# Counting row, rows of x and picked indices read from PSUM in the expert search of a decoder step, with a third buffer for U

## The reference

```
q      = x_t @ w_q                                  # two halves of 128
s1, s2 = scores of the halves against 128 keys each
(s1,i1), (s2,i2) = top 16 of each;  c = top 16 of the 256 sums s1 + s2
e      = 128 * i1 + i2                              # expert, one of 16384
g      = softmax(c)
out_t  = sum over the 8*16 picks of  g * gelu(u[e] . x_t) * v[e]
```

## Time and profile before

| | us |
|---|---|
| median of three runs | 3584.55 (3582.04 to 3585.8) |
| the profiled execution | 3597.29, with a span of 3595.5 |
| PE busy | 3243.4 (90%) |
| DVE busy | 1916.3 (53%) |
| ACT busy | 1366.5 (38%) |
| POOL busy | 1044.5 (29%) |

### The profile page before, as it was taken

One profiled execution on the slowest core, in us unless ns is written; L12 is line 12 of the kernel. 1 busy time (PEld: TensorE's weight loads), 2 busy tenths in 40 slices (PEclk: granted clock), 3 DMA queues, 4 the chain that ended last, 5 costly groups with the idle time before them and its releaser, 6 DMA issues. The chain is left out here.

```text
span 3595.5 us, 53340 instructions
## 1 busy us (share of the span) xinstructions
PE 3243.4 (90%) x21256; PEld 3009.4 (84%) x21256; DVE 1916.3 (53%) x2438; ACT 1366.5 (38%) x1708; POOL 1044.5 (29%) x537
## 2 busy tenths in 40 slices
PE   7999997968879888499979998988888999999998
PEld 6999996757778788499979998988888978888886
DVE  5344443432311000465355888887898567777765
ACT  5333322113522232343334444465676433333332
POOL 0000000004532353000023888877667601111100
PEclk9999997668988798799989999998999999999999
DMA  6555552325453542366765788778777978888864
GB/s 203 173 165 165 165 165 87 105 74 169 146 171 132 176 142 78 119 204 203 180 132 141 177 225 205 202 209 247 244 198 240 304 282 316 295 322 296 304 238 152
DMA packets 446567, 696.65 MB, mean 194 GB/s; under 512 B 30205, under 2 KB 342813, under 8 KB 418878
## 3 DMA queue, kind: packets, MB, share of 16 engines
q1 hardware_dynamic: 397086, 554.35, 49.4%
q10 hardware_dynamic: 40128, 73.42, 7.3%
q0 software_dynamic: 9216, 67.11, 4.8%
HBM read 627.94 MB, written 63.70 MB: 192 GB/s over the span
## 5 line engine op out<-in xcount | busy, mean ns | idle before, releaser
L2422 POOL TENSOR_TENSOR peer_uT_low<-peer_uT,peer_uT_high 128x1024 fp32r<-128x1024 f32 x256 | 680.8, 2683 | 316.1 <-ACT peer_uT_high L2449 314.7
L961 POOL TENSOR_TENSOR gate_low<-gate_raw,gate_high 128x512 fp32r<-128x512 f32 x192 | 244.9, 1301 | 1177.1 <-ACT gate_high L917 1177.0
L2325 PE MATMUL banks<-x_high,peer_uT_high 128*128 128x256 f32 x2048 | 515.3, 291 | 22.9 <-ACT peer_picks_T L2479 13.3
L2326 PE MATMUL banks<-x_low,peer_uT_high 128*128 128x256 f32 x2048 | 508.7, 288 | 0.0
L2325 PEld LDWEIGHTS banks<-x_high,peer_uT_high 128*128 128x128 f32 x2048 | 403.7, 197 | 24.6 <-ACT peer_uT_high L2449 19.0
L2326 PEld LDWEIGHTS banks<-x_low,peer_uT_high 128*128 128x128 f32 x2048 | 402.4, 196 | 0.0
L2574 DVE STREAM_TRANSPOSE peer_uT<-peer_u 128x1024 f32<-128x1024 f32 x256 | 310.7, 1229 | 149.5 <-DMA peer_u<-in_peer_u_dram 141.2
L228 PE MATMUL banks<-x_high,win_high 128*128 128x288 f32 (+1 forms) x1312 | 349.1, 296 | 0.0
L229 PE MATMUL banks<-x_low,win_high 128*128 128x288 f32 (+1 forms) x1312 | 348.7, 295 | 0.0
L2449 ACT ACTIVATE peer_uT_high<-peer_uT 128x1024 fp32r<-128x1024 f32 x256 | 265.0, 1056 | 204.4 <-DVE peer_uT L2574 203.1
L198 ACT ACTIVATE win_high<-win_raw 128x2048 fp32r<-128x2048 f32 x84 | 160.8, 1914 | 334.9 <-DVEq L191 329.4
(11 more groups left out here) (377 smaller groups left out, 6891.3 us busy)
## 6 DMA issues: line engine op xcount, KB each, us to landing
win_raw<-in_w_in_dram SPq DMA_DIRECT2D x38, 2048.0 KB, 8.1
peer_u<-in_peer_u_dram SPq DMA_DIRECT2D x256, 256.0 KB
peer_u<-in_peer_u_dram ACTq DMA_DIRECT2D x256, 256.0 KB
peer_u<-in_peer_v_dram SPq DMA_DIRECT2D x64, 1024.0 KB, 5.2
peer_area<-in_peer_v_dram SPq DMA_DIRECT2D x64, 1024.0 KB, 5.4
gate_raw<-in_w_in_dram SPq DMA_DIRECT2D x96, 512.0 KB, 3.9
w_raw<-in_w_up_ret_dram SPq DMA_DIRECT2D x8, 2048.0 KB, 9.5
w_raw<-in_w_out_dram SPq DMA_DIRECT2D x8, 2048.0 KB, 8.1
```

The source lines that it names most:

```text
L961: pool.tensor_tensor(self.low[:, p % 2, c, :, :], self.raw[:, p % 4, :, c * P:(c + 1) * P], self.high[:, p % 2, c, :, :], ALU.subtract).th ...
L2325: pe.matmul(out, UH[:, c, k, :], XH[:, k, 0:DENSE], start=(k == 0), stop=False)
L2326: pe.matmul(out, UH[:, c, k, :], XL[:, k, 0:DENSE], start=False, stop=False)
L2422: pool.tensor_tensor(UL[:, m % 2, part, :], UT[:, m % 2, part, :], UH[:, m % 2, part, :], ALU.subtract).then_inc(low, 1)
```

## The change

- x's rows are copied by ACT once, in block 28, into banks 0 to 3 (PXROWS); the dots read them there. The SBUF space that they leave becomes a third buffer of U from block 30 on (`THIRD_FROM`), so that a load is issued three blocks ahead of its use.
- The counting row is copied once to bank 7 (PIOTA), and the list IXF is written to bank 7. DVE's comparisons, products and hot rows read these from PSUM.
- The plain one-hots move from ACT (five instructions for a spread) to DVE (one 128x512 comparison). The weighted ones are made by `tensor_scalar` instead of `scalar_tensor_tensor`.
- All spreads go to bank 6, so a spread waits until the one before it is kept. Of two spreads in a block the second stands between the high and the low matmuls.
- The first dots lie in halves 64 to 129 instead of 52 to 129. PE waits for all dots ahead of the output stage, which writes banks 0 to 3.

```
-DOTS = ((52, 130, SLOTS * 3 // 16), (130, 248, SLOTS - SLOTS // 8 if SPARSE > NEW else SLOTS))
+THIRD_FROM = 30
+DOTS = ((64, 130, SLOTS * 3 // 16), (130, 248, SLOTS))
...
+        def u_block(m):
+            slot = m % 2 if m < THIRD_FROM else m % 3
+            return (U[:, slot, :] if slot < 2 else XROWS).rearrange("p (E d) -> p E d", E=4)
+        PXROWS = PS[:, 0:4, :].rearrange("p b n -> p (b n)")
+        PIOTA, IXF = PS[:, 7, 0:P], PS[:, 7, P:P + GR * TOPK].rearrange("p (g k) -> p g k", k=TOPK)
...
+        def u_loads_after(m):
+            if m < THIRD_FROM:
+                return [m + 2]
+            return [n for n in ((m + 2, m + 3) if m == THIRD_FROM else (m + 3,)) if n < BLOCKS]
...
@@ spread (PE)
-                    pe.wait_ge(w_ready, after(q - 1))
+                    pe.wait_ge(w_ready, after(q))
...
@@ hidden (PE)
                         pe.matmul(out, UH[:, c, k, :], XL[:, k, 0:DENSE], start=False, stop=False)
+                    for q in between:
+                        spread(q)
...
-                    for q in spread_at(m):
+                    for q in spread_at(m)[:1]:
                         spread(q)
-                    hidden(m // 2, m % 2)
+                    hidden(m // 2, m % 2, spread_at(m)[1:])
...
@@ scalar
-                def second(q):
...
+                act.activation(PIOTA, iota[:], ACT.Copy).then_inc(iota_ready, 1)
...
+                                act.activation(PXROWS, XROWS, ACT.Copy).then_inc(xrows_moved, 1)
...
@@ dot (DVE)
-                    dve.tensor_tensor_reduce(out=ROWS[:, g % 4, :], in0=ROWS[:, g % 4, :], in1=XROWS, scale=1.0, scalar=0.0,
+                    dve.tensor_tensor_reduce(out=ROWS[:, g % 4, :], in0=ROWS[:, g % 4, :], in1=PXROWS, scale=1.0, scalar=0.0,
...
@@ hot_rows (DVE)
                     dve.wait_ge(placed, after(q - 1))
+                    dve.tensor_tensor(SECOND[:, b, :, :], PIOTA.unsqueeze(1).to_broadcast([P, 4, P]),
+                                      SEL[:, 1, 4 * q:4 * q + 4].unsqueeze(2).to_broadcast([P, 4, P]),
+                                      ALU.is_equal).then_inc(second_ready, 1)
                     for j in range(4):
                         t = 4 * q + j
-                        ins = dve.scalar_tensor_tensor(out=FIRST[:, b, j, :], in0=iota[:], scalar=SEL[:, 0, t:t + 1],
-                                                       in1=SEL[:, 2, t:t + 1].to_broadcast([P, P]), op0=ALU.is_equal, op1=ALU.mult)
+                        ins = dve.tensor_scalar(FIRST[:, b, j, :], PIOTA, SEL[:, 0, t:t + 1], SEL[:, 2, t:t + 1],
+                                                ALU.is_equal, ALU.mult)
```

More of the change, by code:

```diff
@@ L2176, in peer @@
         SECOND, FIRST = (shared[:, k * 8 * P:(k + 1) * 8 * P].rearrange("p (b j n) -> p b j n", b=2, j=4) for k in range(2))
-        temporaries = itertools.accumulate((0, 256, 256, 256, 128, 128, 256, 256, 128), lambda at, n: at + n, initial=A_MU)
-        next(temporaries)
-        BEST, IX, IXF = (view(next(temporaries), (GR, TOPK), "p (g k) -> p g k", k=TOPK) for _ in range(3))
+        temporaries = itertools.accumulate((256, 256, 128, 128, 256, 256, 128), initial=A_MU)
+        BEST, IX = (view(next(temporaries), (GR, TOPK), "p (g k) -> p g k", k=TOPK) for _ in range(2))
         TS, J = (view(next(temporaries), (PEER_HEADS, TOPK), "p (h k) -> p h k", k=TOPK) for _ in range(2))
@@ L2218, in peer @@
             "second_ready", "first_ready", "placed", "weights_ready", "weights_stored")
-        turned, uT_high, low, hidden_done, gelu_ready, distances = st.sems(
-            "turned", "uT_high", "uT_low", "hidden_done", "gelu_ready", "distances")
+        turned, uT_high, low, hidden_done, gelu_ready, iota_ready, xrows_moved = st.sems(
+            "turned", "uT_high", "uT_low", "hidden_done", "gelu_ready", "iota_ready", "xrows_moved")
         u_loaded = st.sems(*(f"u_loaded{r}" for r in range(4)))
@@ L2242, in _, with load_u @@
             def _(sp):
-                def load_u(m):
-                    sp.wait_ge(turned, after(2 * (m - 2) + 2))
+                def load_u(m, turned_block):
+                    if m == THIRD_FROM + 2:
+                        sp.wait_ge(xrows_moved, after(1))
+                    sp.wait_ge(turned, after(2 * turned_block + 2))
                     load_quadrants(sp, m, (0, 1))
@@ L2260, in store_gelu @@
                     sp.dma_start(S["gelu"][m], GE[:, m % 4, :]).then_inc(ge_stored[m % 4], 16)
-                load_u(0)
+                load_quadrants(sp, 0, (0, 1))
                 sp.dma_start(iota[:], C["iota"]).then_inc(iota_loaded, 16)
-                load_u(1)
+                load_quadrants(sp, 1, (0, 1))
                 for m in range(BLOCKS):
-                    if m + 2 < BLOCKS:
-                        load_u(m + 2)
+                    for n in u_loads_after(m):
+                        load_u(n, m)
                     if m >= 3:
@@ L2316, in _, with hidden @@
             def _(pe):
-                def hidden(s, c):
+                def hidden(s, c, between=()):
                     m = s * 2 + c
@@ L2356, in spread @@
                     pe.wait_ge(second_ready, after(q + 1))
-                    pe.wait_ge(w_ready, after(q - 1))
+                    pe.wait_ge(w_ready, after(q))
                     for j in range(4):
-                        last = pe.matmul(PS[:, 6 + b, j * P:(j + 1) * P], SECOND[:, b, j, :], FIRST[:, b, j, :], start=True, stop=True)
+                        last = pe.matmul(PS[:, 6, j * P:(j + 1) * P], SECOND[:, b, j, :], FIRST[:, b, j, :], start=True, stop=True)
                     last.then_inc(placed, 1)
@@ L2402, in four @@
                         output(g * 4 + b, b, b // 2, b % 2, first and b == 0, last and b == 3)
+                pe.wait_ge(used, after(SLOTS))
                 four(0, first=True)
@@ L2449, in high @@
                         act.activation(UH[:, m % 2, part, :], UT[:, m % 2, part, :], ACT.Copy).then_inc(uT_high, 1)
-                    if m + 2 < BLOCKS:
-                        load_quadrants(act, m + 2, (2, 3))
+                    for n in u_loads_after(m):
+                        if n == THIRD_FROM + 2:
+                            act.wait_ge(xrows_moved, after(1))
+                        load_quadrants(act, n, (2, 3))
                 def gelu(m):
@@ L2496, in keep @@
                     act.activation(W[:, :, 4 * n:4 * n + 4].rearrange("p i t -> p t i"),
-                                   PS[:, 6 + q % 2, :].rearrange("p (t i) -> p t i", t=4), ACT.Copy).then_inc(w_ready, 1)
+                                   PS[:, 6, :].rearrange("p (t i) -> p t i", t=4), ACT.Copy).then_inc(w_ready, 1)
                 def split_v(n):
@@ L2513, in _ @@
                 high(0)
+                act.wait_ge(iota_loaded, after(16))
+                act.wait_ge(keys_ready, after(4))
+                act.activation(PIOTA, iota[:], ACT.Copy).then_inc(iota_ready, 1)
                 keep_scores(0)
@@ L2521, in _ @@
                             keep_scores(t)
+                            if t == 2:
+                                act.wait_ge(scores_ready, after(3))
+                                act.activation(PXROWS, XROWS, ACT.Copy).then_inc(xrows_moved, 1)
                         if m == EXPS_AT[t]:
@@ L2574, in turn @@
                     dve.transpose(UT[:, m % 2, b * HALF:(b + 1) * HALF, :].rearrange("p c (E e) -> p E c e", E=4),
[L2575 removed]
+                                  u_block(m)[:, :, cols].rearrange("p E (c i) -> p E c i", i=32)).then_inc(turned, 1)
                 halves = itertools.count()
@@ L2641, in _ @@
                     dve.tensor_scalar(JJ[:, 1, :], j, 15, None, ALU.bitwise_and).then_inc(steps, 1)
-                    dve.tensor_copy(IXF[:], IX[:]).then_inc(steps, 1)
+                    dve.wait_ge(iota_ready, after(1))
+                    dve.tensor_copy(IXF, IX[:]).then_inc(steps, 1)
                     worked(t, 3 * larger)
```

12 lines of the change are left out of this document (5 added, 7 removed).

## The result

The changed kernel takes 3477.8 us in the median of four runs (3471.9 to 3483.1), the kernel before 3585.2 beside it: a ratio of 0.970, 95% interval 0.968 to 0.972. It is faster by 107 us. The forecast was 3529, 56 us less, in a range of 3485 to 3582. So the direction was right, and the size was too small by half, just outside the range. The profiled execution took 3474.3 us with a span of 3472.5.

The account below looks back on a forecast made before the run. The prediction took DVE, slowed beside POOL by instructions with two SBUF tensors, to bound the blocks with spreads. Savings of 30 (blocks 67 to 127) + 25 (30 to 67) + 1 (0 to 30) = 56 us gave 3529, range 3485 to 3582.

Parts of the forecast that it names:

- the gathers: Blocks 67 to 127: nine dots wait for gathers counted as landing late, 3.5 us each, 32 us in all.
- The floor: Blocks 67 to 127: PE's least time, 339 us of blocks plus 63 spreads at 1.05 us, 405 us.
- The 8 us for splitting: Blocks 67 to 127: 24 pairs of spreads no longer share a start, 0.32 us each, 8 us.
- 6 us for a late keep: Blocks 67 to 127: places where a dot makes ACT's keep of the first spread late, 6 us added.
- 12 us around W: Blocks 67 to 127: loads of U late around three stores of W, 4 us each, 12 in all (0 to 27).
- Durations: DVE instructions reading PSUM: hot row 0.30 us, plain one-hots 0.66 a spread, dot 2.29.
- Blocks 30 to 67: Picks and dots get shorter on DVE, PE becomes the bound: 210 + 7 + 6 = 223 us, 25 less.
- the 6 for picks: Blocks 30 to 67: 6 us added for picks instructions with two SBUF tensors left.
- Blocks 0 to 30: The first group's picks get shorter: 1 us less.
- Rival B: Transfers become the new bound: blocks 67 to 127 take 492 us, 20 gained from picks, 3565 us; chance 0.18.
- Rival A: Gathers come in time and W's rest halves: 94 us less, 3491 us; chance 0.17.
- Rival C: Hot rows: a PSUM operand doesn't free DVE of POOL, +36 us there, -8 in picks, 3613 us; chance 0.09.

Follow-up runs that it names:

- the run with 2: The changed kernel with each gather issued two blocks ahead of its dot instead of four (GATHERS_AHEAD = 2); ratio 0.997 to the kernel before.
- the second execution: The changed kernel itself, unedited, timed and profiled again; ratio 0.967 to the kernel before, stage 795.7 us.

## Why the prediction was wrong

**What bounds the kernel before: right.** DVE was the bound of the blocks with spreads, and its long instructions were those beside POOL with their inputs in SBUF. Undoing the hot rows and the comparison brings the long ones back and costs 57 us. One thing was too narrow: the prediction put the stretch down to two tensors in SBUF, and a `tensor_scalar` with one has it too.

**The step that failed is the gathers.** It put 32 us of new stops into blocks 67 to 127 from a constant misread as 2. Measured, DVE waits for no gather in these blocks at all, and 1.1 us in blocks 30 to 67. The mechanism is real, as the run with 2 shows, but it lies in another kernel. It is the largest of four terms that together were 51 us too many there; without it the forecast would have been 3497, still 19 us over what was measured. The view held a warning: between gather and dot lay at least 13.7 us in the profile of before, which I put down to DVE being late.

**The other terms of that stretch.** Forecast 405 + 6 + 32 + 12 = 455, measured 404.1:

- The floor was 405 and is 395. I took 1.05 us for every spread, also for those of a split pair. By the gelus of blocks 73 and 74 after (2379.25 and 2385.79) it costs 6.54 - 5.65 = 0.89, and a split pair 7.44 - 5.65 = 1.79, no more than two together. The 8 us for splitting were not there, and the lone ones give the other 2. In before a lone one did take 1.06 by the gelus; what makes it shorter now I did not find out.
- 6 us for a late keep: 0.3 here, 3.7 in the second execution.
- 12 us around W: 404.1 - 395 = 9 are left over the floor. Right, and the idle time for U is where it was foreseen, around W. The place in the changed kernel's DVE timeline, block 82, is the one named, a load behind W's 4 MB, and the dot and the hot rows behind that load:

```profile
2426.21 1.25 DVE L2587 STREAM_TRANSPOSE peer_uT<-peer_area 128x1024 f32<-128x1024 f32 x1 [5.60 <-DMA peer_area<-in_peer_u_dram]
2427.38 2.25 DVE L2578 CUSTOM_DVE_ANT_0 peer_area<-peer_area,banks 128x2048 f32<-128x2048 f32 x1
```

**Durations.** Dots: 2.29 forecast, 2.25 measured. One-hots: 0.66 and 0.67. Hot rows: 0.30 and 0.40, but four of them take 1.35 us together since they overlap, so the sum for DVE was about right.

**Blocks 30 to 67: right,** 223 against 220.4, with 10.6 us at blocks 44 and 64 where I had 7 (7.6 in the second execution, which takes 217.4), and nothing of the 6 for picks. Two terms that miss in opposite directions cancel in part. **Blocks 0 to 30** gave 4.7 us, not 1. All of it lies in blocks 15 to 20, beside the first group's picks: by the gelus these six take 38.6 us before and 33.9 after, and the longer of the two products with the list there took 4.12 us and now takes 2.25. That accounts for some 2 us at most; how the rest comes about I did not follow.

**Rival B** saw the transfers filled, and they are, at 0.93. But PE hardly waits: with three buffers, and gathers issued four blocks ahead, the longer landings are covered. **Rival A** was the nearest, at 3491. With the spread's true price its sum is 10 us less, 3481, against 3478 measured. Part of that closeness is luck: for the stage the same sum gives 808 us, and the trace has 798. **Rival C** fell with the first look at the hot rows.

## What to carry to other kernels

Beside a busy POOL, look at the longest and the mean duration of each VectorE line and not at the shortest: an operand moved to PSUM can be slower by itself (401 ns against 336) and still free an engine. When a fast engine replaces a slow one, price the next waits with the constants of the code read again and with the landing times of a fuller machine: a gather went from 6.6 to 10.0 us, and DVE's waiting for loads with two buffers from 79 to 120. Parts of one change may only pay together: here the one bank, the split pair and the one-hots off ACT.

## What the runs showed that I had not expected

The granted clock of PE rose from 0.93 to 1.00 in blocks 67 to 127 once its stops were gone. The transfers run at a share of 0.93 to 0.96 for 600 us with PE busy for 98% of them, though a gather then needs 10.0 us instead of 6.6. And storing W one block earlier, with the same bytes, makes the stage 14 us longer in the one execution profiled, and 9 by the medians, where the intervals overlap.
